# Attention that computes its scores once: probabilities with queries on the partitions, turned and split in two, against values in two parts

## The reference

```python
def gqa_attend(q, k, v):            # 6 query heads, 2 key/value heads, 64 wide
    s = jnp.einsum('bqkgd,bskd->bkgqs', qi, k).astype(jnp.float32) * (HEAD_DIM ** -0.5)
    p = jax.nn.softmax(s, axis=-1).astype(v.dtype)
    return jnp.einsum('bkgqs,bskd->bqkgd', p, v)

def diff_attend(q, k, v, lam):      # 4 heads, two maps of 32 each, values 64 wide
    s = jnp.einsum('bqhmd,bshmd->bhmqs', qi, k).astype(jnp.float32) * (DIFF_HD ** -0.5)
    p = jax.nn.softmax(s, axis=-1)
    a = (p[:, :, 0] - lam * p[:, :, 1]).astype(v.dtype)
    return jnp.einsum('bhqs,bshe->bqhe', a, v)
```

## Time and profile before

| | |
|---|---|
| time, median of 3 runs | 2792.62 us (2789.35 to 2808.73) |
| the profiled execution: its own time | 2789.06 us |
| its span in the trace | 2787.4 us |
| PE busy | 2454.5 us (88%) |
| DVE / ACT / POOL busy | 1361.0 / 969.4 / 322.8 us |
| layer 0: preparing stage, main stage of attention | 405.2 to 438.5 us, 439.5 to 639.0 us |
| layer 1: main stage of attention | 1605.5 to 1802.9 us |

### The profile page before, as it was taken

The page is one execution under the profiler, slowest core; times in us unless marked ns, Lnnn a source line. Parts: engine busy times, 40 slices in busy tenths (PEclk is TensorE's granted clock), DMA queues, the critical chain, the costliest instruction groups (busy, mean ns, idle before and its releaser), DMA issues. The chain is left out here.

```text
span 2787.4 us, 44962 instructions
## 1 busy us (share of the span) xinstructions
PE 2454.5 (88%) x18566; PEld 2125.1 (76%) x18566; DVE 1361.0 (49%) x1939; ACT 969.4 (35%) x1492; POOL 322.8 (12%) x362
## 2 busy tenths in 40 slices
PE   5996788998899999989948699884899999999993
PEld 4984564557899999989836645484799999999992
DVE  5576564344422222246656724442554555455556
ACT  4332232352421122143222424421444444344443
POOL 0055231100000000000643420001000000000002
PEclk8997997999999999989978979995899999999997
DMA  5333750443122322223157000012865676667654
GB/s 211 96 78 76 215 166 0 177 200 91 53 73 64 92 64 69 66 53 98 33 116 202 19 0 1 23 38 76 257 211 170 200 233 207 183 211 217 197 180 167
DMA packets 432689, 340.35 MB, mean 122 GB/s; under 512 B 93969, under 2 KB 397535, under 8 KB 428319
## 3 DMA queue, kind: packets, MB, share of 16 engines
q1 hardware_dynamic: 415967, 277.43, 34.0%
q10 hardware_dynamic: 11520, 41.95, 4.6%
q0 software_dynamic: 5056, 18.88, 1.7%
HBM read 287.68 MB, written 50.53 MB: 121 GB/s over the span
## 5 line engine op out<-in xcount | busy, mean ns | idle before, releaser
L2253 PE MATMUL ps<-h_hi,w_hi 128*128 128x256 f32 x1408 | 399.8, 284 | 5.6 <-DVE w_lo L2336 5.6
L2253 PE MATMUL ps<-h_hi,w_lo 128*128 128x256 f32 x1408 | 399.4, 284 | 0.0
L2253 PE MATMUL ps<-h_lo,w_hi 128*128 128x256 f32 x1408 | 399.3, 284 | 0.0
L2336 DVE TENSOR_TENSOR w_lo<-w_raw,w_hi 128x2048 fp32r<-128x2048 f32 (+1 forms) x180 | 309.2, 1756 | 120.5 <-ACT w_hi L2286 120.5
L2253 PEld LDWEIGHTS ps<-h_hi,w_hi 128*128 128x128 f32 x1408 | 271.0, 192 | 8.7 <-issue 6.0
L2253 PEld LDWEIGHTS ps<-h_lo,w_hi 128*128 128x128 f32 x1408 | 271.0, 192 | 2.8
L2253 PEld LDWEIGHTS ps<-h_hi,w_lo 128*128 128x128 f32 x1408 | 270.9, 192 | 0.0
L2286 ACT CAST w_hi<-w_raw 128x2048 fp32r<-128x2048 f32 (+1 forms) x180 | 256.6, 1474 | 2.6 <-DMA w_raw<-in_moe_w_down 2.6
L1790 DVE TENSOR_REDUCE max<-ps 128x1 f32<-128x768 f32 (+1 forms) x140 | 115.5, 825 | 217.1 <-PE ps L1690 131.6
L1855 ACT ACTIVATE tm<-ps 128x512 f32<-128x512 f32 (+1 forms) x196 | 105.1, 551 | 202.7 <-PE ps L1720 126.9
L2555 PE MATMUL ps<-ffn_h_hi,w_hi_ffn 128*128 128x320 f32 x704 | 161.9, 311 | 5.5 <-DVE ffn_h_lo L378 4.2
(11 more groups left out here) (421 smaller groups left out, 5281.9 us busy)
## 6 DMA issues: line engine op xcount, KB each, us to landing
w_raw<-in_moe_w_gu SPq DMA_DIRECT2D x182, 512.0 KB
w_raw<-in_moe_w_down SPq DMA_DIRECT2D x91, 512.0 KB
G_decay<-in_ada_w ACTq DMA_DIRECT2D x54, 512.0 KB, 4.5
w_ahead<-in_ffn_w_gu SPq DMA_DIRECT2D x44, 512.0 KB, 5.2
slots_h<-zeros SPq DMA_DIRECT2D x13, 1024.0 KB, 13.3
slots_y<-zeros SPq DMA_DIRECT2D x12, 1024.0 KB, 26.5
w_ahead<-in_ffn_w_down SPq DMA_DIRECT2D x16, 704.0 KB, 4.7
oA<-in_ada_w ACTq DMA_DIRECT2D x20, 512.0 KB, 5.1
```

Source lines behind the costliest of these rows:

```text
L2253: mm = pe.matmul(ps[:, j % 2, half * BLK:(half + 1) * BLK], gu(wt, j, half, k), x[:, k, :], start=(k == 0 and n == 0), stop=(k == KC - 1 a ...
L2336: dve.tensor_tensor(wlo[:, q, part], raw[:, q, part], whi[:, q, part].bitcast(F32), ALU.subtract).then_inc(s["lo_d" if down else "lo_u"], 1)
```

## The change

The scores are computed once, with queries on the partitions. The scale and a minus sign go into the query (for B into the norm's gain, for C into the split), so DVE takes a minimum. ACT takes the exponential over the whole row of 768 keys from PSUM, with the minimum as its per-partition bias, and the same instruction gives the row sum (`accum_out`), so the column of ones is gone. PE transposes the probabilities in blocks of 128x128: 25 per unit, in seven *steps* (`STEPS`; the first has one block, each of the others four) through the ring of two PSUM banks. ACT copies the hi part of a step (`split_hi`), DVE the lo part (`split_lo`). The values are split once too, hi and lo side by side as 128 stationary columns, and `weigh` streams `p_hi` and then `p_lo` in the fast format; the two halves of its output rows are added by a matmul with `fold`, which replaces the transposes of `turn_out`. `key_major`, `turn_max`, `max_rows` and POOL's copies are gone. In the order, v is the unit being turned; v+1 has its scores made, v-1 is weighed.

In the preparing stage the token tiles come before the cached keys, whose loads (and those of the cached values and `lv`) now start in this stage; `lv` is waited for by DVE at its head; ACT takes over half of DVE's `kC` copies. The zeros now come from a source of 1 KB a partition, repeated 8 times.

```diff
...
+                    pool.tensor_scalar(gqk[:, 0], gqk[:, 0], -HD ** -0.5, None, ALU.mult).then_inc(s["gain_in"], 1)
...
-            kBlo = sb("kB_lo", [P, KVB, KEYS], F32R)
+            kBlo = sb("kB_lo", [P, KEYS], F32R)
-                slB = sbi("split_lB", [P, 2, KVB, HD + 2], F32R)
+                slB = sbi("split_lB", [P, 2, KVB * HD], F32R)
...
-                items = [("cache", 0), ("cache", 1)] + [("new", t) for t in range(NT)]
+                items = [("new", t) for t in range(NT)] + [("cache", 0), ("cache", 1)]
...
+                        dve.wait_ge(s["lv_in"], 16)
...
+                            act.wait_ge(s["turned_c"], n + 1)
+                            act.copy(kC[0:RC, 0:4, k0:k0 + P], bank[5][0:RC]).then_inc(s["out_ck"], 1)
...
+            vB = sb("vB", [P, NK, KVB, 2, HD], F32R)
+            vC = sb("vC", [P, NK, HC, 2, HD], F32R)
+
+            def value_parts():
+                for v, cv, c0, n in ((vB, cvB, VB0, KVB), (vC, cvC, VC0, HC)):
+                    new, old = (x.rearrange("p t (h d) -> p t h d", d=HD) for x in (tm[:, :, c0:c0 + n * HD], cv))
+                    for k0, k1, x in ((0, 1, new[:, 0:1]), (1, 3, old), (3, NK, new[:, 1:NT])):
+                        yield v[:, k0:k1, :, 0], v[:, k0:k1, :, 1], x
...
+            STEPS = ((-1, ()), (0, ((0, 0), (0, 1), (0, 2), (0, 3))), (1, ((1, 0), (1, 1), (1, 2), (1, 3))),
+                     (1, ((0, 4), (1, 4), (0, 5), (1, 5))),
+                     (2, ((2, 0), (2, 1), (2, 2), (2, 3))), (3, ((3, 0), (3, 1), (3, 2), (3, 3))),
+                     (3, ((2, 4), (3, 4), (2, 5), (3, 5))))
+            NS = len(STEPS)
...
+                    if l == 0:
+                        pool.memset(zero, 0.0).then_inc(s["zeroed"], 1)
+                    for n, (hi, lo, x) in enumerate(value_parts()):
+                        pool.wait_ge(s["v_hi"], n + 1)
+                        pool.tensor_tensor(lo, x, hi.bitcast(F32), ALU.subtract).then_inc(s["v_lo"], 1)
...
-                                sp.dma_start(slots[r * BLK:(r + 1) * BLK].rearrange("(p a) d -> p (a d)", a=2), zero[:]
-                                             ).then_inc(s["filled"], 16)
+                                sp.dma_start(slots[r * BLK:(r + 1) * BLK].rearrange("(p a) (b d) -> p (a b) d", a=2, d=256),
+                                             bcast_mid(zero, 8)).then_inc(s["filled"], 16)
...
-                            pe.wait_ge(s["smax"], n - 1)
+                            pe.wait_ge(s["p_in"], n - 1)
...
+                    def turn(u, j):
+                        n = NS * u + j
+                        pe.wait_ge(s["p_in"], NT * u + STEPS[j][0] + 2)
+                        if n >= 2:
+                            pe.wait_ge(s["lo"], n - 1)
+                        if j == 0:
+                            pe.transpose(ring(n)[:, 0:P], prob_slot(u, 0), self.ident).then_inc(s["turned"], 1)
+                            return
+                        for q, (t, k) in enumerate(STEPS[j][1]):
+                            mm = pe.transpose(ring(n)[:, q * P:(q + 1) * P], prob_block(u, t + 1, k), self.ident)
+                        mm.then_inc(s["turned"], 1)
...
+                            pe.wait_ge(s["lo"], NS * (u + 1))
+                            if u == 0:
+                                pe.wait_ge(s["v_lo"], NV)
                             if u:
                                 pe.wait_ge(s["o_sb"], u)
-                        p0 = k * 4 * P
-                        mm = pe.matmul(ps[0:V1, OB, :], v[:, k + 1, g, :], pT[:, u % 2, p0:p0 + 4 * P],
-                                       start=(k == 0), stop=(k == NKL - 1))
+                        for n, part in enumerate((p_hi, p_lo)):
+                            mm = pe.matmul(ps[:, OB, :], values(u, k + 1), part[:, k * 4 * P:(k + 1) * 4 * P],
+                                           start=(k == 0 and n == 0), stop=(k == NKL - 1 and n == 1))
...
+                            mm = pe.matmul(ps[:, XB, P + t * HD:P + (t + 1) * HD], oT[:, (t - 1) * P:t * P] if t else oTc, fold,
+                                           start=True, stop=True)
...
+                    for v in range(-1, NU + 1):
+                        ahead, now, done = v + 1 < NU, 0 <= v < NU, v >= 1
+                        if ahead:
+                            scores(v + 1, 0)
+                            scores(v + 1, 1)
+                        if done:
+                            for k in range(4):
+                                weigh(v - 1, k)
+                        if ahead:
+                            scores(v + 1, 2)
+                        if done:
+                            for k in range(4, NKL):
+                                weigh(v - 1, k)
+                        if now:
+                            for j in range(3):
+                                turn(v, j)
+                        if ahead:
+                            scores(v + 1, 3)
+                        if now:
+                            turn(v, 3)
+                        if done:
+                            turn_out(v - 1)
+                        if now:
+                            turn(v, 4)
+                        if ahead:
+                            scores(v + 1, 4)
+                        if now:
+                            weigh_context(v)
+                            turn(v, 5)
+                            turn(v, 6)
...
+                    def least(u, t):
+                        dve.wait_ge(s["scores"], NT * u + t + 1)
+                        dve.tensor_reduce(low[:, u % 2, t:t + 1], score_tile(u, t), AX.X, ALU.min).then_inc(s["least"], 1)
+
+                    def split_lo(u, j):
+                        n = NS * u + j
+                        dve.wait_ge(s["hi"], n + 1)
+                        dve.tensor_tensor(place(p_lo, j), turned(n), place(p_hi, j).bitcast(F32), ALU.subtract).then_inc(s["lo"], 1)
...
+                    for v in range(-1, NU + 1):
+                        ahead, now, done = v + 1 < NU, 0 <= v < NU, v >= 1
+                        if ahead:
+                            for t in range(3):
+                                least(v + 1, t)
+                        if now:
+                            for j in range(3):
+                                split_lo(v, j)
+                        if ahead:
+                            least(v + 1, 3)
+                        if now:
+                            split_lo(v, 3)
+                        if done:
+                            if v - 1 == HB:
+                                dve.wait_ge(s["gated"], 3 * NT)
+                            out(v - 1)
+                        if now:
+                            split_lo(v, 4)
+                        if ahead:
+                            least(v + 1, 4)
+                        if now:
+                            split_lo(v, 5)
+                            split_lo(v, 6)
...
+                    def probabilities(u, t):
+                        act.wait_ge(s["least"], NT * u + t + 1)
+                        n = 4 * u + t - 1
+                        if t == 0 and u >= 2:
+                            act.wait_ge(s["turned"], NS * (u - 2) + 1)
+                        if t and n >= PR:
+                            u0, t0 = divmod(n - PR, 4)
+                            act.wait_ge(s["turned"], NS * u0 + (4, 4, 7, 7)[t0])
+                        if t and n == PR - 1:
+                            act.wait_ge(s["v_lo"], NV)
+                        x = score_tile(u, t)
+                        act.activation(prob_slot(u, t), x.rearrange("p (a n) -> p a n", a=3) if t else x, ACT.Exp, scale=-1.0,
+                                       bias=low[:, u % 2, t:t + 1], accum_out=rs[:, u % 3, t:t + 1]).then_inc(s["p_in"], 1)
...
+                    def split_hi(u, j):
+                        n = NS * u + j
+                        act.wait_ge(s["turned"], n + 1)
+                        if u and j == 0:
+                            act.wait_ge(s["pv"], u)
+                        if j == NS - 1:
+                            act.wait_ge(s["pvc"], u + 1)
+                        act.copy(place(p_hi, j), turned(n)).then_inc(s["hi"], 1)
+
                     def bring_out(u):
                         act.wait_ge(s["pv"], u + 1)
-                        if u >= 2:
-                            act.wait_ge(s["o_turned"], u - 1)
-                        act.copy(oT[:, u % 2, P:T], ps[0:V1, OB, :]).then_inc(s["o_sb"], 1)
-                        act.wait_ge(s["ring_in"], context_item(u) + 1)
-                        act.copy(oT[:, u % 2, 0:P], ps[0:V1, 4 + context_item(u) % 2, 0:P]).then_inc(s["ring_out"], 1)
+                        if u:
+                            act.wait_ge(s["o_turned"], u)
+                        else:
+                            act.wait_ge(s["v_lo"], NV)
+                        act.copy(oT, ps[:, OB, :]).then_inc(s["o_sb"], 1)
+                        act.wait_ge(s["pvc"], u + 1)
```

(67 more changed lines are left out.)

272 lines of the change are left out of this document (96 added, 176 removed).

## The result

The changed kernel takes 2920.7 us (median of 4 runs, 2917.2 to 2928.7), the kernel before 2792.3 in the same comparison: ratio 1.045, 95% interval 1.0405 to 1.0497. The forecast was 2858 with a range of 2828 to 2912: the direction is right, the size is off by 63 us, and the result lies 9 us outside the range. The profiled execution took 2917.2 us, 128 more than that of before.

A forecast was written before the change was run, and what follows sets the result against it. The prediction took PE's order to be late before, and a chain of hand-overs between engines to bind after. Main stages add 32.3 us per layer, 65 for two, on the 2792.6 median: 2858 us, range 2828 to 2912.

The forecast's parts named there:

- The chain: Main stage: hand-overs between PE, ACT and DVE in program order set each round, 14.8 us with C scores, 15.9 with B.
- eight C rounds: Main stage, rounds with C scores, the mixed one included: 8 x 14.8 = 118.4 us against 83.05 before, +35.3 a stage.
- The clock: PE in C rounds: idle 6 us a round in pieces of at most 2.4, granted clock expected at 1.00.
- the chain's first link: Start of a C round: eight fast weighing matmuls and the score tile with its drain, 2.2 us.
- Rival (c): C rounds: clock falls to 1.2 GHz without float32 weighing, 18.5 us a round, +59, total 2917 us; chance 12%.
- The opening: Main stage's start, 50.5 us before, then one B round of 15.9: -2 us taken, bounds -4 and +4 for the clock.
- zero fill: Zero writes, now in 1 KB packets: hidden behind the stage unless below 115 GB/s, costed at nothing.
- tail: Main stage after the last scores: 17.2 us, no change.
- B score tile: PE in B rounds: a tile keeps its 1.45 us; its 64-partition matmuls change nothing there.
- Preparing stage: Stage before attention's main stage: fewer DVE copies against a wait for `lv`, net -2 to +3 us a layer, taken as 0.
- D: Theory stated after the result, for the main stage: a plain sum of work on one engine sets the round; no size given.
- rival (a): Main stage: waits do not bind, PE's saving shows, -18.5 us a stage, total 2756; needs C rounds below 10.4; chance 5%.

The follow-up runs named there:

- Run 5: Changed kernel with the same instructions and waits in another order on PE, DVE and ACT, plus a fourth buffer of row sums: 2786.9 us, ratio 0.9967.
- run 1: Changed kernel with 13 useless 512-column fast matmuls a round added on PE, in gaps where it waits: 2872.9 us, ratio 1.0269.
- Run 9: Changed kernel with the second matmul of each B score block on all 128 partitions in place of 64: 2883.0 us, ratio 1.0310.
- run 10: Changed kernel reordered, with weighing's first wait one step earlier, `lv` used later, row sums before the last copy, and 128-partition second B matmuls: 2728.8 us, ratio 0.9749.
- Runs 2: Changed kernel with one wait moved: `weigh(u, 0)` waits for `split_lo` step 5, only `weigh(u, 4)` for step 6: 2898.0 us, ratio 1.0372.
- run 7: Changed kernel with only the preparing stage altered: `lv` products and ACT's small exponential later, row sums before the last copy: 2921.5 us, ratio 1.0460.
- run 3: Changed kernel without the lo part of the probabilities: no `split_lo`, one weighing matmul a block in place of two: 2859.2 us, ratio 1.0218.

## Why the prediction came out as it did

**The chain sets a round: right.** Run 5 shows it best: another order of the same instructions takes 65 to 71 us off the stage, 48 to 49 of them at equal clock. At full clock (run 1) the eight C rounds took 119.3 and 118.1 us (forecast 118.4). Two B rounds and the mixed one took 48.2; the forecast's 3 x 15.9 = 47.7 is near it partly by luck, since a B round came 0.7 longer and the mixed one, 14.9, was in fact priced like a C round by the links.

**The clock: the step that failed.** It read "After the change PE idles 6 us in each C round, in pieces of at most 2.4, so I expect 1.00 in it". The idle was about so (4.6 us, in pieces of up to 1.8, in the round shown), but the clock was 0.5 in four tenths of a C round, the part that holds the chain's first link. Against run 1 that is 131.5 - 119.3 = 12.2 us for the eight C rounds of layer 0, and 51.3 - 48.2 = 3.1 for the three rounds ahead of them; in layer 1 13.5 and 8.2. Together this is 37 of the 63 us. The row of 1.00 in a stage of transposes was right, and it does hold for the turning here (1.00 from 658.5 to 665.5); it says nothing of what comes after idle time. The Trainium skill, TensorE: Matmul & The Clock Gate, Part 4, named there, is again not borne out on transposes: the turning, which holds them with a few score tiles and folds between, is the part of the round that has full clock. Rival (c) gave 2917 and was priced at 12%: its effect is what happened, but it came on part of each round (1.6 us, not 3.7), and run 1 shows that the missing float32 weighing was not needed for full clock, only denser work. That its total lies 4 us from the measured one is luck: the B rounds and the opening, which it left alone, brought the rest.

**The opening: mis-sized.** Forecast: 48.5 us up to the end of the first B round (50.5 - 2, bounds -4 and +4 on the difference). The forecast's rounds run from first weighing to first weighing, and by its links ACT's copy comes 5.7 us behind that in a B round and 4.6 in a C round. So the forecast for the second copy is 54.2; measured 444.82 to 507.86, 63.0, and 61.5 in layer 1, which has no zero fill, so the fill is not the reason. "Five score tiles cost the same" holds (10.7 us in both), but the first B round took 22.6 us at a clock of 0.57, not 15.9, and the round ahead of it, with turning and score tiles in turn, ran at 0.50 to 0.62. I had the clock back with the first weighing, as it was in the earlier trace rows; fast weighing brought it back for some microseconds only. Run 1, whose filler stands in later rounds for the most part, still took 61 for these steps with a clock of 0.50 in their first 40 us, so this term is apart from that of the C rounds. Run 9 took 48.0, with a clock of 1.00 from 465 us on: there the clock came up without float32 weighing, once the score tiles' matmuls all had one height.

**The sum.** Layer 0, against the forecast of 231.8, from copy to copy: opening +8.8, the three rounds behind it +4.7 (46.6 by the links), C rounds +13.1, tail +2.3 (14.9 for 17.2 - 4.6; 1.3 of it is where the window ends): 28.9 in all, or 260.7. Layer 1 took 264.4, against 229.7, where a second B round was at 22.5. The two layers together miss by 63.6 us, 2.3 of them the windows' ends; with the preparing stages (+6) and everything else (-4) that is the 63 of the result.

**Parts that were right or small.** Prices of instructions: all within 0.03 us. DVE's and ACT's work in a C round: 8.6 to 9.3 and 8.3, forecast 9.2 to 9.9 and 9.0. Zero fill: hidden, as said; its 25 transfers took 11 us each, and the last landed some 80 us into the stage. B score tile 1.45: right at full clock; that "its 64-partition matmuls change nothing there" is right for the change, but run 10 shows what they cost, some 0.67 us a tile. Preparing stage: 36.3 and 35.9 for 34.3 and 32.0 before, so +2 and +4, at or just over the bound of +3: the load of `lv` held DVE until 412.55, 4.0 us after ACT began, not 2.3. Everything outside these stages differs by -3.6 in all between the two profiles. Runs 2 and 5 speak against D and rival (a) as long as the order is that of the change. Rival (a)'s turning point, a C round of 10.4 us, was too strict: run 5 has 11.0 and a B round of 13.0, and comes out 0.3% ahead.

**What stays open.** Why the clock falls in some C rounds of the reordered kernels and not in others; how much of the opening's 8.8 us is clock and how much is its steps, since no run has it at full clock in the order of the change with the tiles of two heights; and why run 7's gain does not show in its median.

## What to carry to other kernels

When each engine waits for another and none is full, price the order before the work: here a new order of the same steps was worth 134 us, some 48 of them (run 1) through the clock, and moved a loss of 4.5% to a gain of 0.3% (0.2 to 0.5); with one wait moved, a loaded table used later and full-height matmuls the gain is 2.5%. When a change opens gaps on PE, price its links at 1.2 GHz as a case of its own, with the links that stand right behind the gaps first; some useless matmuls in those gaps are a cheap test of it. Matmuls of different heights one after another should be looked at for their distance, not their share of busy time.

## What was unexpected of the hardware

- Adding 3 us of matmuls a round made the kernel 48 us faster (2920.7 to 2872.9): the granted clock went from 0.82 to 0.97 in the C rounds of layer 0.
- PE with full records can stay at 1.2 GHz: 78 of 82 us busy at 0.52 (run 3), 36 of 38 at 0.57 to 0.62 (after, opening, 470 to 507.86), while a kernel with fewer busy microseconds had 1.00 in the same steps (run 9, 7.25 of 10).
- A 128-partition and a 64-partition matmul of 512 columns that alternate start 0.41 to 0.43 us apart at full clock; both at 128 partitions, 0.32 and 0.23.
- The delta scan of layer 0, with the same code in all kernels after, took from 176 to 187 us from one profile to the next.
